# Down weights of the expert two ahead issued from ScalarE's queue, gate and up weights from SyncE's

## The reference

```python
def moe_ffn(x, w_router, router_bias, w_gate, w_up, w_down):
    ...
    h = jax.nn.silu(jnp.einsum("td,edf->tef", t, w_gate)) * jnp.einsum("td,edf->tef", t, w_up)
    h = h * gates.astype(h.dtype)[..., None]
    return jnp.einsum("tef,efd->td", h, w_down).reshape(B, L, D)
```

## Time and profile before

| what | us |
|---|---|
| median of 3 runs | 681.05 |
| lowest, highest | 679.89, 682.53 |
| the profiled execution, whole time | 680.64 |
| its span | 678.8 |
| PE busy in the span | 595.5 (88%) |
| DMA mean over the span | 261 GB/s |

### The profile page before, as it was taken

The page is one execution under the profiler, slowest core; times in us unless marked ns, Lnnn a source line. Parts: engine busy times, 40 slices in busy tenths (PEclk is TensorE's granted clock), DMA queues, the critical chain, the costliest instruction groups (busy, mean ns, idle before and its releaser), DMA issues.

```text
span 678.8 us, 15190 instructions
## 1 busy us (share of the span) xinstructions
PE 595.5 (88%) x6783; PEld 468.4 (69%) x6783; DVE 246.5 (36%) x493; ACT 142.9 (21%) x255; POOL 61.1 (9%) x89
## 2 busy tenths in 40 slices
PE   2789999999999998799757999999999999999900
PEld 0475544566666557644446999999999999999800
DVE  2560748888746645310666000000000000000126
ACT  1330453333147301100240211111111111110012
POOL 1046000000030100020001100000000000100030
PEclk9899999999999999799885999999999999999965
DMA  8989430303303808940996899999999999999263
GB/s 273 392 300 359 161 125 0 125 1 124 125 5 110 329 0 303 326 100 12 394 394 209 305 389 391 395 391 402 394 399 392 387 391 394 395 411 408 94 211 124
DMA packets 80793, 177.15 MB, mean 261 GB/s; under 512 B 5992, under 2 KB 12911, under 8 KB 80367
## 3 DMA queue, kind: packets, MB, share of 16 engines
q1 hardware_dynamic: 64848, 149.01, 58.9%
q0 software_dynamic: 5728, 17.96, 8.0%
q10 hardware_dynamic: 10175, 9.56, 4.3%
HBM read 164.06 MB, written 12.47 MB: 260 GB/s over the span
## 4 chain that ended last, share of the span: by engine, by line
PE 50%; issue 3%; DMA 2%; DVE 1%; POOL 1%; ACT 1%; DVEq 0%; POOLq 0%; ACTq 0%
PE psum L852 21%; PE psum L849 17%; PE psum L777 5%; PE psum L860 2%; PE psum L784 2%; DMA h_rows<-ye 1%; PE psum L866 1%; POOL slot L1150 1%; PE psum L791 1%; DMA xe<-h_rows,lst 1%; PE psum L437 1%; PE psum L763 1%; DMA y_rows<-ye 1%; DVE XS L1922 0%; DVE XS L1885 0%
## 5 line engine op out<-in xcount | busy, mean ns | idle before, releaser
L852 PE MATMUL psum<-slot,xeTa 128*32 128x128 f32 x1536 | 171.8, 274 | 0.0
L849 PE MATMUL psum<-slot,xeTa 128*32 128x384 f32 x1536 | 169.9, 489 | 0.5 <-ACT xeTa L1420 0.5
L852 PEld LDWEIGHTS psum<-slot,xeTa 128*32 128x32 f32 x1536 | 168.4, 111 | 0.3
L525 PE MATMUL psum<-hT,slot 128*128 128x384 f32 x304 | 100.8, 489 | 0.0
L849 PE MATMUL psum<-slot,heT 128*32 128x384 f32 x768 | 85.8, 487 | 1.9 <-issue 1.4
L852 PE MATMUL psum<-slot,heT 128*32 128x128 f32 x768 | 86.8, 273 | 0.0
L525 PEld LDWEIGHTS psum<-hT,slot 128*128 128x128 f32 x304 | 56.9, 190 | 38.2
L852 PEld LDWEIGHTS psum<-slot,heT 128*32 128x32 f32 x768 | 82.6, 110 | 0.0
L849 PEld LDWEIGHTS psum<-slot,xeTa 128*32 128x32 f32 x1536 | 68.9, 109 | 0.8 <-ACT xeTa L1420 0.6
L534 PE MATMUL psum<-slot,hT 128*128 128x512 f32 x96 | 42.3, 595 | 0.6 <-DMA slot<-in_w_in 0.6
L2057 DVE COPY ye<-psum 128x384 f32<-128x384 f32 x16 | 8.9, 557 | 90.1 <-PE psum L852 90.1
(11 more groups left out here) (385 smaller groups left out, 699.7 us busy)
## 6 DMA issues: line engine op xcount, KB each, us to landing
slot<-in_w_gate SPq DMA_DIRECT2D x16, 2048.0 KB, 18.9
slot<-in_w_up SPq DMA_DIRECT2D x16, 2048.0 KB, 19.6
slot<-in_w_down SPq DMA_DIRECT2D x16, 2048.0 KB, 18.9
slot<-in_w_ada SPq DMA_DIRECT2D x12, 2048.0 KB, 13.5
slot<-in_w_in SPq DMA_DIRECT2D x7, 2048.0 KB, 8.6
y_rows<-ye ACTq DMA_DIRECT2D x16, 288.0 KB, 6.4
slot<-in_w_out SPq DMA_DIRECT2D x2, 2048.0 KB, 16.6
y_rows<-T POOLq DMA_DIRECT2D x7, 384.0 KB, 13.3
```

Source lines behind the costliest of these rows:

```text
L525: last = mm(o[:, 0:TOK], w[:, kt, tile(i)], hT[:, kt, :], start=(kt == 0), stop=(kt == KT - 1))
L849: mm(psum[32 * g:32 * g + 32, bank, 0:PACK], x(k, g), w(k)[:, 0:PACK], start=(k == 0), stop=(k == terms - 1), tile_position=(0, 32 * g))
L852: last = mm(psum[96:128, bank, tile(g)], x(k, g), w(k)[:, PACK:CW], start=(k == 0 and g == 0), stop=(k == terms - 1), skip_group_check=Tru ...
```

## The change

In the loop and at its end SP no longer asks for down weights. ACT does, for expert n+2, directly behind its wait for `down_done` of n, ahead of its copy of y(n). The first two experts' weights and the branch for overflow rows stay as they were.

```diff
                     n = 2 * it + p
                     reload(n, p, 1, it)
                     reload(n + 1, 1 - p, 0, it + p)
-                    reload(n, p, 2, it)
             reload(E - 2, 0, 1, E // 2 - 1)
             reload(E - 1, 1, 0, E // 2 - 1)
-            reload(E - 2, 0, 2, E // 2 - 1)
             reload(E - 1, 1, 1, E // 2 - 1)
-            reload(E - 1, 1, 2, E // 2 - 1)
...
+            def load_down(n, p):
+
+                dst = slot[home(p, 2)][:, :, :].rearrange("p k n -> p (k n)").rearrange("p (k d) -> p k d", d=D)
+                src = A["w_down"][0, n] if isinstance(n, int) else A["w_down"][0, bass.ds(n, 1)].rearrange("o a b -> (o a) b")
+                act.dma_start(dst, src.rearrange("(k p) d -> p k d", p=P)).then_inc(loaded[home(p, 2)], 16)
+
...
                     act.wait_ge(s["down_done"], n + 1)
+                    if not last_pair:
+                        load_down(n + 2, p)
                     if not first:
                         act.wait_ge(s[f"y_out{p}"], 32 * it)
```

## The result

| | before | after |
|---|---|---|
| median of 4 runs each, us | 680.47 | 688.95 |
| lowest, highest | 678.90, 682.53 | 687.82, 690.28 |
| span of the profiled execution | 678.8 | 686.6 |
| PE busy | 595.5 | 597.6 |

The changed kernel takes 1.0124 times as long, with a 95% interval of 1.0089 to 1.0158: 8.5 us more, where the prediction had 7.

The account below looks back on a forecast made before the run. The prediction took PE to set the pace in the experts, with the DMA engines full. Its terms, 0 + 0 + 0 + 7 = 7 us, put the median of 681.05 at 688.0 us, range 682 to 695.

Parts of the forecast that it names:

- The bound: Stage of the experts: PE sets the pace, with 2.1 us of waits in all; DMA engines are full, share 1.04.
- Issues on SP and ACT: Fourteen down-load issues leave SP, worth 0; fourteen are added on ACT at 0.4 us each, hidden, so 0.
- transfers behind the new load: Writes of y queued behind 2 MB on ACT's queue, and POOL's gathers, land later but in time: 0.
- Order of the transfers: Down loads on their own queue overtake gate loads, so PE waits: 6.1 us worked out, bounds 3.4 and 8.8, 7 taken.
- new place: Landing time a gate load takes over from the down load that overtakes it: gate(13) 587.4, gate(14) 606.4.
- the clock: Stalls of PE of a few us should not lower the granted clock; 1.5 us kept in the range.
- The 7 us taken: Cost of the transfer order in the experts, chosen between the equal share's 6.1 us and the upper bound of 8.8.
- The margins hold: Rival, chance 0.19: two deep queues raise the DMA rate 2.7% during the backlog, so no loss, 681 us.
- Down weights starve: Rival: ACT's queue gets under a fifth, down(13) lands 7.6 us late; 689 to 695 us; chance 0.15 including a lower rate.
- SP's issuing was the limit: Rival, chance 0.02: loads get going sooner without SP's long issues; gains at most 2.1 us, 679 us.
- The rule of turns: DMA engines go round-robin between queues; with one piece per turn, the stall sum is 6.9 to 8.8 us, not 6.1.

Follow-up runs that it names:

- half loads: Changed kernel, but each of ACT's down loads moves only the first half of the rows (1 MB): 682.55 us, ratio 0.9992.
- the holds: Kernel before, PE held ahead of gate(15) by chained DVE copies: ten (long) 688.94 us, ratio 1.0087; four (short) 684.73 us, ratio 1.0023.
- half-size pieces: Changed kernel, each down load issued as two of 1 MB, with 2 KB pieces instead of 4 KB: 689.18 us, ratio 1.0094.

## Why the prediction was right, point by point

**The bound.** Right. PE set the pace and the engines that move data had nothing to spare; their share stayed at 1.04 over the 226 us of growing backlog. Without the backlog the change costs nothing (0.9992).

**Issues on SP and ACT, transfers behind the new load: 0.** Right. ACT's issues took 0.40 us, as estimated; the copy of y starts 0.5 us later and nobody waits for it. The half loads show all three items at once at no cost.

**Order of the transfers.** The mechanism is right: what is overtaken lands later, and PE waits for it. The sum is right too, 6.1 us against 5.9 in the trace (1.20 + 1.16 + 3.56), but the way to it isn't, so that the closeness is in part luck. Down loads took 12.2 us, some 206 GB/s of 400 with the landing taken off, which is the half that was assumed. The working gave the whole stall to gate(13), and said of gate(14) that it adds nothing. Here are gate(13) in the changed kernel and up(13) in the kernel before:

```profile
L999 SPq DMA_DIRECT2D slot<-in_w_gate x1: 9722/9722/9722, 556.8 to 556.8; - x1
DMA to landing us min/median/max: 29.4/29.4/29.4
...
L999 SPq DMA_DIRECT2D slot<-in_w_up x1: 2389/2389/2389, 571.8 to 571.8; - x1
DMA to landing us min/median/max: 23.7/23.7/23.7
```

gate(13) was in time: 556.8 + 29.4 = 586.2, needed at 587.0. It landed about at its new place, 587.4; the 4.6 us that it was to lose on top, as sharing with down(13), it didn't lose. gate(14) in turn landed at 608.8, 2.4 us behind its new place, 606.4: down(14) had been asked for at 598.97 and not at 604.0, since PE was less late than worked out. The stalls are at gate(12), up(13) and gate(14). Up loads I had not listed at all, and up(13) had the smallest margin of all: it landed at 571.8 + 23.7 = 595.5 and was needed at 603.0 - 5.24 = 597.8. That is 2.3 us, against gate(14)'s 2.4.

**The step that was mis-sized: the clock.** "Stalls of a few us should cost no clock", with 1.5 us kept in the range. It cost 2.0 us behind the 3.56 us stall, and 1.8 and 1.9 in the holds. The earlier trace rows was the wrong neighbour: 5 us at 1.00 with PE idle, but the clock falls right behind it, where nothing runs on PE and it costs nothing:

```profile
650.00:655.00 5.00, 0.00 (x0) 0.00 (x0) 0.00 (x0) 0.00 (x0) 3.86 (x4) 0.50 0.56 164
```

**The 7 us taken.** It was put above 6.1 because 6.1 supposes that gate(13) takes all of it at once. gate(13) took nothing, three loads shared the stall, and the sum was still not above 6.1. That 7 lies near 8.5 is due to this surcharge of 0.9 standing in for the 2 us of the clock: luck.

**The rivals.** *The margins hold* needed 2.7% more rate; it is 394 against 393 GB/s. *Down weights starve*: they landed in 12 us; a wait for them never came. Of *SP's issuing was the limit* nothing was seen: SP's issues are up to 9.7 us long in the changed kernel as well, with a third fewer of them, since they mirror the backlog.

**The rule of turns.** With one piece per turn ACT's queue would get two thirds, and down loads would have landed in about 10 us; they took 12.2. By the half-size pieces the share does depend on the piece, but it is 206 against 163 GB/s, where one piece per turn would give 267 against 200. The sum by that rule, 6.9 to 8.8, doesn't hold for the stalls. The Trainium skill, DMA: Bandwidth & Descriptors, section Queues, rings and completion order, has each DMA engine take turns between queues by packets; the runs here agree with turns, but not with a turn of one piece.

**Left open.** Why gate(13) lost nothing by sharing with down(13); why 4.2 us of stall went with 1 MB, where the working says 2.7; and what tells a 2 us stall that lowers the clock from one that doesn't.

## What to carry to other kernels

When the DMA engines are full and the loads are asked for in the order in which they are used, a second queue was no help in any form tried here: it lets one stream overtake, and the streams that are needed sooner pay. Read the margin of every load (landing against first use), not of one kind alone, before moving any; here margins of 2 to 7 us were too small, where one load takes 5.4 us to move. And a load held back while the engines still have room is paid for later, 200 us on in this case, so what helped against overtaking was fewer bytes in the critical stretch, with the loads held back only once the backlog was there.

## What the hardware showed that was not expected

A stall of PE can cost clearly more than its length from some 2 us on: 1.7 to 2.0 us on top, with 3 to 4 us at a granted clock of 0.50, in all four stalls of 3.35 to 4.37 us and in three of seven of 1.99 to 2.64. Thirty stalls of 1.2 to 1.9 us in two kernels cost 0.2 us on top. By these numbers splitting one long stall into two short ones would be worth an estimated 1.3 to 1.6 us, which wasn't tried. And ACT's queue got half of the moving for a 2 MB load in 4 KB pieces beside SP's 2 KB ones, but two fifths with 2 KB pieces.
